# The front of a hybrid decoder layer on one core: modulation rows by one-column matmuls, h pair by pair, and two attention units beside the gates

## The reference

```python
mod = silu(c) @ w_ada + b_ada                 # w_ada: 1024 x 3072
shift, scale, gate = split(mod, 3)
h = rmsnorm(x, norm_w) * (1 + scale) + shift
proj = h @ w_in                               # w_in: 1024 x about 11,000
aq, ak, av, az, mq, mk, mv, mo, mz, mi, mf, ga, gm = split(proj)
aq, ak = rope(aq, positions), rope(ak, positions)
y_att = (sliding_window_attention(aq, ak, av, sinks) * silu(az)) @ w_att
y_m = (mlstm(conv(mq), conv(mk), mv, mi, mf) * sigmoid(mo) * silu(mz)) @ w_m
x = x + gate * ((sigmoid(ga) * y_att + sigmoid(gm) * y_m) @ w_out)
return rmsnorm(x, final_norm_w)
```

## Time and profile before

| | us |
|---|---|
| median of three runs | 1391.82 |
| lowest and highest | 1391.68, 1391.87 |
| the profiled execution's own time | 1391.64 |
| its span, from first to last instruction | 1389.9 |
| TensorE matmuls busy | 1328.2 (96%) |
| TensorE weight loads busy | 1128.8 (81%) |
| VectorE busy | 668.1 (48%) |
| GpSimd busy | 662.6 (48%) |
| ACT busy | 397.0 (29%) |
| DMA | 89.30 MB, mean 64 GB/s |

### The profile page before, as it was taken

The page is one execution under the profiler, slowest core; times in us unless marked ns, Lnnn a source line. Parts: engine busy times, 40 slices in busy tenths (PEclk is TensorE's granted clock), DMA queues, the critical chain, the costliest instruction groups (busy, mean ns, idle before and its releaser), DMA issues.

```text
span 1389.9 us, 20009 instructions
## 1 busy us (share of the span) xinstructions
PE 1328.2 (96%) x6846; PEld 1128.8 (81%) x6846; DVE 668.1 (48%) x1297; ACT 397.0 (29%) x926; POOL 662.6 (48%) x854
## 2 busy tenths in 40 slices
PE   3499999999999999999999999999999999999997
PEld 2398797989877888889978987898789888688886
DVE  5979886785873000153265235424542321544335
ACT  5334445353450100023322332333132311311111
POOL 6834507061366544295267146715661455557340
PEclk9799999999999999999999999999999999999999
DMA  9411102010021220230131031103210132321502
GB/s 350 123 45 31 47 2 61 15 32 28 0 61 61 75 79 26 89 93 17 48 89 30 0 90 46 30 0 92 59 30 15 45 92 91 106 91 61 197 16 106
DMA packets 119832, 89.30 MB, mean 64 GB/s; under 512 B 13305, under 2 KB 111721, under 8 KB 118894
## 3 DMA queue, kind: packets, MB, share of 16 engines
q1 hardware_dynamic: 116288, 76.16, 17.9%
q10 hardware_dynamic: 3502, 12.61, 2.6%
HBM read 80.35 MB, written 8.41 MB: 64 GB/s over the span
## 4 chain that ended last, share of the span: by engine, by line
PE 82%; DVE 12%; issue 2%; ACT 2%; DVEq 0%; ACTq 0%
PE pp L532 24%; PE pp L533 23%; PE pp L534 23%; PE pp L718 2%; PE pp L728 2%; PE pp L638 1%; DVE y_lo L1294 1%; DVE prob L1237 1%; DVE num L1404 1%; PE pp L710 1%; PE pp L621 1%; PE pp L629 1%; PE pp L723 1%; PE pp L622 1%; PE pp L607 1%
## 5 line engine op out<-in xcount | busy, mean ns | idle before, releaser
L484 POOL TENSOR_TENSOR w_hi<-raw,ones 128x256 fp32r<-128x256 f32 x404 | 284.1, 734 | 619.1 <-ACTq L346 341.0
L532 PE MATMUL pp<-h_hi,w_hi 128*128 128x512 f32 x912 | 361.5, 396 | 9.9 <-DVE h_lo L1120 8.3
L533 PE MATMUL pp<-h_lo,w_hi 128*128 128x512 f32 x912 | 356.1, 390 | 0.0
L534 PE MATMUL pp<-h_hi,w_lo 128*128 128x512 f32 x912 | 355.9, 390 | 0.0
L488 POOL TENSOR_TENSOR w_lo<-raw,w_hi 128x256 fp32r<-128x256 f32 x404 | 345.7, 887 | 7.9
L532 PEld LDWEIGHTS pp<-h_hi,w_hi 128*128 128x128 f32 x912 | 171.8, 188 | 49.6 <-issue 6.8
L534 PEld LDWEIGHTS pp<-h_hi,w_lo 128*128 128x128 f32 x912 | 171.8, 188 | 36.0
L533 PEld LDWEIGHTS pp<-h_lo,w_hi 128*128 128x128 f32 x912 | 171.9, 188 | 34.6
L532 PE MATMUL pp<-w_hi,h_hi 128*128 128x384 f32 (+1 forms) x512 | 162.1, 317 | 0.6 <-DVE roped L1214 0.6
L534 PE MATMUL pp<-w_hi,h_lo 128*128 128x384 f32 (+1 forms) x512 | 158.1, 309 | 0.0
L533 PE MATMUL pp<-w_lo,h_hi 128*128 128x384 f32 (+1 forms) x512 | 158.0, 309 | 0.0
(11 more groups left out here) (216 smaller groups left out, 1855.9 us busy)
## 6 DMA issues: line engine op xcount, KB each, us to landing
raw<-w_in SPq DMA_DIRECT2D x72, 512.0 KB, 3.6
w_mod<-w_ada SPq DMA_DIRECT2D x7, 1024.0 KB, 11.5
x_in<-x SPq DMA_DIRECT2D x4, 1024.0 KB, 8.0
raw<-w_att SPq DMA_DIRECT2D x8, 512.0 KB, 5.0
merged_dram<-mix_a ACTq DMA_DIRECT2D x8, 512.0 KB, 2.6
w_gate<-w_ada ACTq DMA_DIRECT2D x8, 512.0 KB, 3.4
raw<-w_m SPq DMA_DIRECT2D x8, 512.0 KB, 3.6
mix_in<-merged_dram ACTq DMA_DIRECT2D x8, 512.0 KB, 3.3
```

The source lines that it names most:

```text
L484: ins = pool.tensor_tensor(hi[:, q, :], raw[:, s, q, :], one[:, q, :], ALU.mult)
L532: pe.matmul(o, lh, rh, start=first, stop=False)
L533: pe.matmul(o, lh, rl, start=False, stop=False)
L534: return pe.matmul(o, ll, rh, start=False, stop=last)
```

## The change

It rebuilds the front, on all engines.

- SP issues the seven vector loads and the positions ahead of x, and the frequencies behind it, on a semaphore of its own (pos_loaded). w_ada comes in four pairs of feature tiles, for each pair one load of the shift columns and one of the scale columns (1 MB, rows of 1 KB). Between the pairs it loads the first three slots of w_in. The fourth pair lies where x_in was and waits until all of x is transposed. Sinks and gate biases come last.
- GpSimd makes its first constants ahead of the semaphore counters, and the masks behind the reciprocal roots. The gate weights are cleared and split 64 columns wide. Slots 0 to 2 are split at once, slots 3 and 4 only when all of h_lo is there.
- TensorE makes the modulation rows: silu(c) is the stationary operand, one column for each of the eight row tiles, and 256 columns of w_ada stream past. The shift row goes to partition 0, the scale row to partition 64. ACT and VectorE copy one row each into mod_row, and two transposes turn them into columns.
- h is made pair by pair: VectorE scales xnt in place, ACT copies it to h_hi, VectorE subtracts. The gate product of a pair comes one pair later.
- Attention units 0 and 1 run tile by tile between the gate matmuls: six tiles of both, then gate tiles 6 and 7, then the last two tiles of both.
- The mean square is scaled within ACT's square, the epsilon is added on VectorE, one angle step stands behind each scaled block, and the gate biases are added by ACT.
- The residual x loads reuse the x_loaded semaphores, so their waits are for 32 on the first four.

The diff, cut to its core:

```diff
-        w_mod = place("w_mod", [P, KT, 2 * D], F32, HT)
+        w_mod = [place(f"w_mod{f}", [P, 2, KT, 2 * P], F32, offset)
+                 for f, offset in enumerate((HT + K32, HT + K32 // 2, HT + K32 + K32 // 2, YO))]
...
 SP
-            for n in range(4):
-                sp.dma_start(x_in[:, 2 * n:2 * n + 2, :], x_v[:, 2 * n:2 * n + 2, :]).then_inc(x_loaded[n], 16)
             for rows, v, n in (... seven vectors ...):
                 sp.dma_start(vec_rows[rows:rows + n, :], v.rearrange("(r p) -> r p", p=P)).then_inc(vec_loaded, 16)
+            sp.dma_start(pos_i[:, :], ...).then_inc(pos_loaded, 16)
+            for n in range(4):
+                sp.dma_start(x_in[:, 2 * n:2 * n + 2, :], x_v[:, 2 * n:2 * n + 2, :]).then_inc(x_loaded[n], 16)
+            sp.dma_start(freq[:, :], ...).then_inc(pos_loaded, 16)
+            def load_mod(f):
+                for a in range(2):
+                    src = w_ada_v[:, :, a * D + f * 2 * P:a * D + (f + 1) * 2 * P]
+                    sp.dma_start(w_mod[f][:, a, :, :], src).then_inc(mod_loaded[2 * f + a], 16)
+            load_mod(0)
             ... mi and mf columns into slot 4 ...
+            sp.dma_start(raw[:, 0, :, :], w_in_v[:, :, AQ:AQ + P]).then_inc(slot_loaded[0], 16)
+            load_mod(1)
+            sp.dma_start(raw[:, 1, :, :], w_in_v[:, :, AQ + P:AQ + 2 * P]).then_inc(slot_loaded[1], 16)
+            load_mod(2)
+            ... slot 2, in two halves ...
+            sp.wait_ge(x_turned, 16)
+            load_mod(3)
+            ... bias_if, sink ...
...
 GpSimd
+            for s in range(3):
+                split(s, use("A", s, 0), loads("A", s, 2 if s == 2 else 1))
+            pool.wait_ge(h_lo_ready, KT)
+            for s in range(3, 5):
+                split(s, use("A", s, 0), loads("A", s, 1))
...
 TensorE
+            def mod_rows(f):
+                ... f == 0: wait for silu_c_ready, pos_copied; else for both row copies of f - 1 ...
+                for a in range(2):
+                    pe.wait_ge(mod_loaded[2 * f + a], 16)
+                    for k in range(KT):
+                        ins = pe.matmul(pp[64 * a:64 * a + 1, 3, 0:2 * P], silu_c[:, k:k + 1], w_mod[f][:, a, k, :],
+                                        start=(k == 0), stop=(k == KT - 1), skip_group_check=True)
+                ins.then_inc(mod_rows_full, 1)
+            def turn_mod(f):
+                pe.wait_ge(shift_row_out, f + 1)
+                pe.wait_ge(scale_row_out, f + 1)
+                ... two transposes of mod_row into bank 2 ...
+            def gates(k):
+                pe.wait_ge(h_lo_ready, k + 1)
+                for w, h, first, last in ((w_hi, h_hi, True, False), (w_hi, h_lo, False, False), (w_lo, h_hi, False, True)):
+                    for half in range(2):
+                        ins = pe.matmul(pp[0:GATE_COLS, 6 + half, :], w[:, 4, k, 0:GATE_COLS], h[:, k, ...], ...)
+            def early_units(ks):
+                for k in ks:
+                    for u in range(EARLY_UNITS):
+                        ... passes into bank(u), slots 0 to 2 ...
+            for q in range(8):
+                turn_x(q)
+            mod_rows(0)
+            for q in range(8, 12):
+                turn_x(q)
+            turn_mod(0)
+            for q in range(12, 16):
+                turn_x(q)
+            for f in range(1, PAIRS):
+                mod_rows(f)
+                turn_mod(f)
+                for k in range(2 * f - 2, 2 * f):
+                    gates(k)
+            ... wait for the splits of slots 0 to 2 ...
+            early_units(range(0, KT - 2))
+            for k in range(KT - 2, KT):
+                gates(k)
+            early_units(range(KT - 2, KT))
...
 ACT
+            def shift_row(f):
+                act.wait_ge(mod_rows_full, f + 1)
+                act.activation(mod_row[0:1, :], pp[0:1, 3, 0:2 * P], ACT.Copy).then_inc(shift_row_out, 1)
+            for f in range(PAIRS):
+                if f:
+                    shift_row(f)
+                for k in range(2 * f, 2 * f + 2):
+                    act.wait_ge(x_mod_ready, k + 1)
+                    act.activation(h_hi[:, k, :], xnt[:, k, :], ACT.Copy).then_inc(h_hi_ready, 1)
+                if f == 1:
+                    ... the two sines ...
...
 VectorE
+            dve.wait_ge(pos_loaded, 16 * 2)
+            dve.tensor_copy(pos_f[:, :], pos_i[:, :]).then_inc(pos_converted, 1)
+            mean_square(0)
+            for n in range(NB):
+                if n + 1 < NB:
+                    mean_square(n + 1)
+                norm_x(n)
+                angle_step_of(n)
+            angle_step_of(NB)
+            for f in range(PAIRS):
+                ... copy the scale row, wait for mod_turned, three small operations: scale_t, shift, scale1 ...
+                for k in range(2 * f, 2 * f + 2):
+                    dve.wait_ge(x_evac, NB + k + 1)
+                    dve.tensor_scalar(xnt[:, k, :], xnt[:, k, :], scale1[:, k:k + 1], shift[:, k:k + 1], ALU.mult, ALU.add)
+                for k in range(2 * f, 2 * f + 2):
+                    dve.wait_ge(h_hi_ready, k + 1)
+                    dve.tensor_tensor(h_lo[:, k, :], xnt[:, k, :], h_hi[:, k, :].bitcast(F32), ALU.subtract)
+                if f == 2:
+                    ... the two cosine steps ...
```

More of the change, by code:

```diff
@@ L492, in loads @@
                 return before(SLOT_DMAS, phase, s) + n
-            split(4, use("G", 4, 0), loads("G", 4, 2))
-            with pool.Fori(0, KVH, 1) as i:
+            gate_one = ones[:, 0:1, None].broadcast_to([P, KT, GATE_COLS])
+            gate_raw, gate_hi, gate_lo = (t[:, 4, :, 0:GATE_COLS] for t in (raw, w_hi, w_lo))
+            pool.wait_ge(slot_loaded[4], 16 * loads("G", 4, 2))
+            pool.tensor_tensor(gate_hi, gate_raw, gate_one, ALU.mult).then_inc(slot_hi[4], 1)
+            after(pool, slot_hi[4], use("G", 4, 1))
+            pool.tensor_tensor(gate_lo, gate_raw, gate_hi.bitcast(F32), ALU.subtract).then_inc(slot_split[4], 1)
+            for s in range(3):
+                split(s, use("A", s, 0), loads("A", s, 2 if s == 2 else 1))
+            pool.wait_ge(h_lo_ready, KT)
+            for s in range(3, 5):
+                split(s, use("A", s, 0), loads("A", s, 1))
+            with pool.Fori(1, KVH, 1) as i:
                 for s in range(5):
@@ L563, in _, with turn_x @@
             pe.transpose(bank(3)[:, 0:NB], pos_f[:, :], ident[0:NB, 0:NB]).then_inc(pos_turned, 1)
-            for q in range(16):
+            def turn_x(q):
                 half, k = q // 8, q % 8
@@ L574, in _ @@
                 ins.then_inc(x_turned, 1)
[L576 to L586, removed]
-                pe.wait_ge(h_lo_ready, k + 1)
[L588 to L591, removed]
@@ new lines, in gates @@
+            def gates(k):
+                if k == 0:
+                    after(pe, slot_split[4], use("G", 4, 1))
+                    pe.wait_ge(x_evac, 16)
+                pe.wait_ge(h_lo_ready, k + 1)
+                for w, h, first, last in ((w_hi, h_hi, True, False), (w_hi, h_lo, False, False), (w_lo, h_hi, False, True)):
+                    for half in range(2):
+                        ins = pe.matmul(pp[0:GATE_COLS, 6 + half, :], w[:, 4, k, 0:GATE_COLS],
+                                        h[:, k, half * HALF:(half + 1) * HALF], start=first and k == 0, stop=last and k == KT - 1,
+                                        skip_group_check=True)
+                if k == KT - 1:
+                    ins.then_inc(gates_full, 1)
@@ new lines, in _ @@
+            mod_rows(0)
[9 more added lines that the diff above has]
+                    gates(k)
+            pe.wait_ge(x_squared, NB)
+            for s in range(3):
+                after(pe, slot_split[s], use("A", s, 1))
+            early_units(range(0, KT - 2))
@@ L829, in gate_row_step @@
                 if n == 0:
+                    act.wait_ge(gates_full, 1)
+                    act.wait_ge(small_loaded, 16 * 3)
+                    for half in range(2):
+                        t = slice(half * HALF, (half + 1) * HALF)
+                        for p0 in (0, 32):
+                            act.activation(row_if[p0:p0 + 4, t], bank(6 + half)[p0:p0 + 4, :], ACT.Identity,
+                                           bias=bias_if[p0:p0 + 4, :]).then_inc(gates_out, 1)
                     act.wait_ge(row_step, 1)
```

219 lines of the change are left out of this document (110 added, 109 removed).

## The result

The changed kernel takes 1398.01 us (median of 5 runs, 1397.29 to 1398.23); the kernel before, run beside it, took 1391.87 (1391.68 to 1392.15). The ratio is 1.0042, with an interval of 1.0029 to 1.0055. The forecast was 1387.5 and faster; the measured time lies in its range of 1383 to 1400, but on the other side of no change.

The account below looks back on a forecast made before the run. TensorE, busy 96% of the span, was taken as the bound, with the front to be won. The third unit at 77.0 in place of 80.5 gave 3.5 us; staying near that, 1391.8 - 4.3 = 1387.5 us, range 1383 to 1400.

Parts of the forecast that it names:

- the mark: Start of the third attention unit on TensorE, 80.49 before, forecast 77.0; its shift was taken as the shift of the end.
- x later, frequencies behind it: Front loads: eight small DMAs ahead move x by 3.0 us; VectorE's first mean square waits for the frequencies until 17.0.
- the norm loop: VectorE's add, scaling and angle step per block: 1.4 us a block, block 3 scaled at 23.1, block 7 at 28.3.
- Modulation rows: TensorE's 16 one-column matmuls for each pair of tiles: 3.5 us a pair, 3.8 with a change of array shape.
- Rounds: VectorE's work for each pair of tiles: 7.7 us, with TensorE's 7.0 hidden below it.
- The step from 33.1 to 37.2: TensorE after pair 0's rows: the other half of the transposes and the two of the row, 4.0 + 0.3 us.
- Gates and early units: Last part on TensorE: gates 4 and 5 end at 62.8, early units' 36 matmuls at 69.1, gates 6 and 7 at 72.0.
- Loss of the early units: Before the third unit, TensorE stands 2.9 us until VectorE's rope returns bank 0; the fourth starts 4.8 after the third.
- Splits and loads: GpSimd's splits of slots 0 to 2 ready at 60, wanted by 62.8; last w_ada pair lands by 50, wanted at 53.7.
- the two rows do not overlap: Rival for the modulation rows: records for rows 0 and 64 run singly, 6.9 + 0.3 us a pair, 1399 us; chance 0.20.
- Its turning point: Time of one row matmul from which the rival without overlap decides: 0.33 us, third unit at 80.7, even.
- The low clock: Rival: one-column matmuls may not hold the full clock; rows 7 us a pair, third unit at 97.5, 1409 us; chance 0.13.

Follow-up runs that it names:

- the best kernel: Frequencies' DMA issued ahead of x, on top of interleaved rows, the gate row put aside and one early unit in place of two: 1378.90 us.
- Blocks of four: Changed kernel with the row group changed after four row matmuls instead of after eight: 1391.03 us, ratio 0.9993.
- the interleaved run: Changed kernel with shift-row and scale-row matmuls issued in turn, one each, instead of all eight of one and then the other: 1388.80 us, ratio 0.9978.
- putting the gate row aside: Changed kernel with the first rope first on VectorE, memsets before the gates are full, row_e, exponential and logarithm right behind that rope: 1393.53 us.
- the last two experiments: Frequencies' DMA ahead of x, on interleaved rows, gate row aside, one early unit: 1378.90 us; then also w_ada's second and third pairs loaded earlier: 1379.44 us.

## Why the prediction was wrong, point by point

**Bound of the kernel before: right; the mark: too early.** Later stages did not change, and the shift of the fourth unit (5.5 us) is that of the span (5.7). The third unit, which the forecast had as its mark, was off by 2.4: the clock had fallen by then, and its cost falls between the third unit and the fourth.

**x later, frequencies behind it: right in place.** Forecast 17.0 for the first mean square, measured 18.22 for the wait's end; the norm loop took some 1.1 us a block in place of 1.4, so that the transposes started at 23.43 (23.1 forecast) and the first eight tiles ended at 28.9 (29.4). I had called it a loss that the cut does not need, without a price: in the best kernel it is 3.8 us.

**Modulation rows: the step that failed.** Forecast 3.5 to 3.8 us a pair, measured 6.15 from start to next start (6.21 to the last end), within the bounds of 1.9 to 6.9. I chose between two rows by likeness and took 64-wide weights that write partitions 0 and 64. In that row the row group changes after four records; here it changes after 16. I had named that under "for it" in the rival and still priced the term as if all 32 records paired. Blocks of four and interleaving show the length of a block to be the cause: 6.21, 4.49 and 3.62 us with 16, 8 and 2 records to a block, all else equal. The price of the error is the interleaved run: third unit 7.4 us earlier, fourth 8.1, time 9.2 less.

**Rounds: right once the rows are.** Forecast 7.7 us, paced by VectorE. With interleaved rows they are 7.5 and 8.0; as the kernel stood, TensorE set them: 6.21 of rows, 0.56 of waiting for the copied row, 0.22 to the first gate and 2.90 of gates make 9.89. The forecast had GpSimd split beside VectorE through almost all of it. In the changed kernel the splits ended at 51.7 and the last two rounds had VectorE undisturbed, which won nothing, as VectorE was not the pace. (The step from 33.1 to 37.2 adds up to 37.4; nothing hangs on it.)

**Gates and early units.** With interleaved rows the gates 4 and 5 ended at 61.1 (62.8 forecast) and the third unit came at 76.18 (77.0 forecast): except for the rows, the sum held within 1 us.

**Loss of the early units: mechanism right, size short.** Forecast 2.9 us of standing; it was 3.82, since the bias adds took 0.70 each, not 0.50, and row_e 1.47, not 1.2. What the sum left out is the clock: the third unit takes 7.1 us to the fourth (4.8 forecast), as it runs for most of it at granted clock 0.50. The standing and the clock together are some 6 us, of which putting the gate row aside gives 4.5 back. So even the interleaved kernel came 1.3 us above the forecast; some of that is that the forecast took 4.3 us off for a sum that gave 3.5.

**Splits and loads: right, they did not bind.** Slots 0 to 2 were ready at 51.7 (60 forecast), and no row matmul waited for w_ada in the changed kernel. They bind only in the last two experiments.

**Rivals.** What happened is the second, "the two rows do not overlap", forecast at 1399 and measured at 1398.0; but only three quarters of its mechanism: 8 of 32 records do overlap. That its time came within 1 us is in part luck: it had the third unit at 87.7, which came at 83.57, and the clock, which it did not have, took back 2.4 us of that. Its turning point (0.33 us a matmul) is too high for the same reason: with blocks of four, at 4.4 / 16 = 0.28, the third unit is 3.6 us earlier than in the kernel before and the time only even (0.9993). The low clock did not come in the rows: it is 1.00 in every window from 28 to 80 us, so one-column matmuls held it. The clock fell later, where no rival had put it.

The Trainium skill, TensorE: Matmul & The Clock Gate, Part 3, says that matmuls start and end strictly in program order, and models matmuls that are packed into one array, by rows or by columns, as starting about 4 ns after one another. The traces agree with the second, with 7 ns between neighbours in the interleaved rows and 4 to 6 in the changed kernel. They speak against the first: in the changed kernel the weight load that waits for the second half of the pair starts at 41.48, behind 12 records of the first row group; the 13th starts beside it, and the last three of that group start up to 42.13, each beside one of the second group. By the rule as I used it nothing would overlap, and a pair would cost 6.9 us; it cost 6.15.

## What to carry to other kernels

When small matmuls are to run beside each other in different columns of the array, issue them in turn, one of each; the row of a trace that shows such overlap holds only for its own order of issue. When two units are brought forward together, look for what hid behind the second: the release of a buffer that was free becomes a standing of the engine that bounds, and the clock can add to it (2.4 us to 3.82 in the changed kernel). After each gain look for the next wait before adding gains up: three of them here were the first softmax, w_ada's second pair and the splits.

## What the runs showed of the hardware

- fp32 matmuls of one column by 256 to partitions 0 and 64 overlap over four records at a change of group: 0.216 us a record alone, two in 0.216 when paired.
- One-column weights held TensorE's granted clock at 1.00 (28 to 70 us). In the changed kernel the clock was 0.50 until 88.6 behind a standing of 3.82 us; standing 2.14 and 2.16 us was followed by 0.50 too, standing 1.39 and 1.41 us was not. Standing 1.47 to 1.49 us near the end of the first round was followed by it in five of eleven profiles.
- At the low clock a unit of 24 matmuls took 6.6 us in place of 4.15; the gap between their starts went from 0.173 to 0.32 for most of it.
- Beside GpSimd's operand splits VectorE is slower: in the changed kernel two scaled tiles took 2.46 us with GpSimd at work (46.99) and 1.54 with it idle (66.34), two low parts 3.36 and 2.36.
